# Differential attention: the two softmax maps are subtracted before they are turned and multiplied

## The chip, the cores and the metric

The kernel is one program on one core of a Trainium2 chip. TensorE (PE in the profile; its weight loads are PEld) multiplies and transposes, VectorE (DVE), ScalarE (ACT) and GpSimd (POOL) work elementwise, and SyncE (SP) issues most DMAs. Each engine runs its own queue in order and waits on semaphores for the others. The metric is the time of one execution on the device in microseconds, the median of several runs.

## The reference

The model is a first block of two layers and a second block of two layers, on 256 tokens of width 1024, all in float32. The change touches the second block alone. Each of its layers has three attentions: a latent one (MLA, 8 heads), a differential one (4 heads with two softmax maps each) and a windowed one (8 heads). The differential one is

```
s = einsum('bqmhd,bkmhd->bmhqk', qb, k) * scale
s = s - slopes[None, None, :, None, None] * dist[:, None, None]
p = softmax(s, axis=-1)
a = p[:, 0] - lam * p[:, 1]
o = einsum('bhqk,bkhd->bqhd', a, v)
...
o_diff = rms_norm(o, g_diff_out) * (1 - lam_init)
```

where m is the map (0 or 1) and h the head. After the attentions come gates (`gates = sigmoid(gate_logits)`), the three branch projections, an output projection, a feed-forward network with a convolution, and an embedding gate.

## The kernel before, in words

Weights are streamed in units of 128x1024 floats, 147 for a layer of the second block, through a ring of 7 slots. ACT rounds a unit to `w_hi` (L682), and DVE (5 of 7 units) or POOL (2 of 7) computes the rest `w_lo` (L686). PE then multiplies three times (hi by hi, hi by lo, lo by hi) for each product. In the attention stage the units of the gates are spread over the work: `gl0` to `gl23` are 24 matmuls each (L720), one unit for each step i.

The attention stage is a loop over i = 0 to 26, written out on PE, DVE and ACT alike. There are 24 items: 0 to 7 are the differential maps, 8 to 15 the windowed heads, 16 to 23 the latent heads. An item is the score matrix of one map, 256x256, held as 128x512. For an item

- PE computes the scores into a PSUM bank, two items at a time up to item 15 (`scores_pair`, L1254), one at a time after that (`scores2`, L1266);
- DVE adds the distance term into the SBUF tile `z2[:, i % 4]`, which the trace calls z (L2502), and takes the row maxima (L2507, L2509), which increments `z_ready`;
- ACT takes the exponential in place with the row sums (L1797), which increments `p_ready`;
- two steps after the item's own, PE turns the tile with four transposes into a bank (`turn2`, L1275), and ACT (even) or DVE (odd) copies it to `p_t` (`read_p2`, L575 and L573);
- three steps after its own, PE multiplies it by the values with eight matmuls (`weigh2`, L1294).

Items 0 to 3 are the first maps of the four heads and sum into the banks `od0` (0 and 1); items 4 to 7 are the second maps and sum into `od1` (2 and 3). At i = 9 and 11 DVE scales both by the reciprocal row sums, the second also by minus lambda (the name `lam[:, 2:3]` holds it with its sign), and at i = 13 it adds them, squares the sum and reduces it for the norm; at i = 17 it applies the norm (L2554 to L2576).

Beside that runs a chain for the latent heads' queries and keys (`qk`). ACT computes the inverse roots at i = 3 and 4 (L1811, `mla_rstd`), behind the exponential of the step. POOL scales each of the two token tiles twice over 1536 columns (L2794, L2798, `mla_scaled`), with its share of `w_lo` in between. DVE applies the rotary embedding in six small operations, `rope(0)` at i = 7 and `rope(1)` at i = 8 (L2523 to L2528, `mla_roped`). At i = 9 PE turns the first heads (`mla_turn`, L1307) and waits for `mla_roped` there.

PSUM has four working banks (4 to 7), handed out in turn by the table `banks2`, in the order in which PE fills them: scores, turned tiles, `gl` and the rest. A use of a bank waits until the use before it was read. What reads `gl{i}` is ACT, at the end of its step i (L1430).

## Time and profile before

| | us |
|---|---|
| median of 3 runs | 1728.37 (1727.63 to 1729.87) |
| the profiled execution | 1727.11 |
| its span, first to last instruction | 1725.3 |
| PE busy | 1653.6 (96%) |
| DVE busy | 1170.4 (68%) |
| ACT busy | 921.4 (53%) |
| POOL busy | 441.4 (26%) |
| mean granted TensorE clock | 0.986 of full speed |

The attention stage of the second block runs from about 821 to 947 us in its first layer (called layer 0 below) and from about 1306 to 1435 us in its second (layer 1). The times below are us from the start of the span. A timeline row gives start and length, and in brackets the engine's idle time before it and who ended it. Consecutive operations on DVE overlap a little: the next one starts some 0.1 us before the recorded end of the one before. The clock is granted to TensorE in two levels, 2.4 GHz (1.00 in the views) and 1.2 GHz; values in between are means over a stretch.

### The profile page before, as it was taken

The page shows a single profiled execution, that of the slowest core. Times are in us where ns is not written, and L with a number is a line of the kernel's source. Part 1 is how long each engine was busy: PE and PEld are TensorE (multiplying, and loading weights), DVE is VectorE, ACT ScalarE, POOL GpSimd, SP SyncE. Part 2 cuts the span into 40 slices and gives each one's busy share as a digit, 9 for nine tenths or more (in the row PEclk, how much of TensorE's full clock was granted, in tenths as well). Part 3 has the DMA queues.
Part 4 walks back from the last instruction along what each step waited for, and adds up shares of the span by engine and source line. Part 5 has one row for each costly group of instructions (what it writes and reads, how often), then busy time and mean ns, then how long its engine had stood idle before and what let it go on. Part 6 is the DMA issues. An engine that isn't in the chain of part 4 may idle for free.

```text
span 1725.3 us, 30143 instructions
## 1 busy us (share of the span) xinstructions
PE 1653.6 (96%) x11354; PEld 1504.2 (87%) x11354; DVE 1170.4 (68%) x1601; ACT 921.4 (53%) x1576; POOL 441.4 (26%) x184
## 2 busy tenths in 40 slices
PE   8989999999988999999999999999999999999997
PEld 6878799989887899978899989999788999899996
DVE  5687754467786545476884877666767856777677
ACT  5664554446645544465655564545755555554445
POOL 2212122212121322224511132222235211222222
PEclk9999999999999999999999999999999999999999
DMA  9432455646523665546333455655554333466653
GB/s 332 157 119 96 161 199 185 201 147 210 162 78 122 220 193 188 191 153 213 113 110 100 140 199 184 215 185 182 180 194 146 110 100 116 161 218 199 207 183 127
DMA packets 82563, 288.74 MB, mean 167 GB/s; under 512 B 9051, under 2 KB 11908, under 8 KB 81924
## 3 DMA queue, kind: packets, MB, share of 16 engines
q1 hardware_dynamic: 77352, 272.58, 48.1%
q10 hardware_dynamic: 5084, 14.37, 2.5%
q8 instruction: 91, 1.49, 0.4%
q14 instruction: 36, 0.29, 0.1%
HBM read 284.81 MB, written 2.11 MB: 166 GB/s over the span
## 4 chain that ended last, share of the span: by engine, by line
PE 62%; DVE 7%; ACT 3%; issue 2%; DVEq 0%; ACTq 0%
PE bank L720 30%; PE bank L737 25%; PE bank L1294 2%; DVE w_lo L686 2%; PE bank L1275 1%; PE bank L1266 1%; ACT w_hi L682 1%; PE bank L765 1%; PE bank L1254 1%; PE bank L1307 0%; DVE qk L2528 0%; PE bank L1186 0%; PE bank L774 0%; PE bank L910 0%; DVE z L2502 0%
## 5 line engine op out<-in xcount | busy, mean ns | idle before, releaser
L686 POOL TENSOR_TENSOR w_lo<-raw,w_hi 128x1024 fp32r<-128x1024 f32 x146 | 375.3, 2570 | 1175.7 <-ACT w_hi L682 1175.7
L686 DVE TENSOR_TENSOR w_lo<-raw,w_hi 128x1024 fp32r<-128x1024 f32 x364 | 558.2, 1558 | 153.9 <-ACT w_hi L682 151.5
L682 ACT ACTIVATE w_hi<-raw 128x1024 fp32r<-128x1024 f32 x510 | 520.0, 1052 | 101.6 <-PE bank L737 46.3
L720 PE MATMUL bank<-x_t_hi,w_hi 128*128 128x256 f32 x1984 | 321.4, 284 | 5.3 <-ACT gl L1430 2.9
L720 PE MATMUL bank<-x_t_hi,w_lo 128*128 128x256 f32 x1984 | 313.9, 280 | 0.0
L720 PE MATMUL bank<-x_t_lo,w_hi 128*128 128x256 f32 x1984 | 313.5, 280 | 0.0
L720 PEld LDWEIGHTS bank<-x_t_hi,w_hi 128*128 128x128 f32 x1984 | 273.9, 190 | 16.8 <-issue 5.1
L720 PEld LDWEIGHTS bank<-x_t_hi,w_lo 128*128 128x128 f32 x1984 | 268.7, 189 | 0.0
L720 PEld LDWEIGHTS bank<-x_t_lo,w_hi 128*128 128x128 f32 x1984 | 268.2, 189 | 0.0
L737 PE MATMUL bank<-w_hi,x_t_hi 128*128 128x512 f32 (+3 forms) x448 | 136.1, 387 | 9.4 <-issue 5.8
L737 PE MATMUL bank<-w_hi,x_t_lo 128*128 128x512 f32 (+3 forms) x448 | 133.5, 381 | 1.5 <-DVE x_t_lo L1962 1.5
L737 PE MATMUL bank<-w_lo,x_t_hi 128*128 128x512 f32 (+3 forms) x448 | 133.2, 380 | 0.0
L737 PE MATMUL bank<-w_hi,hs_hi 128*128 128x512 f32 x352 | 109.4, 392 | 4.0 <-ACT hs_hi L1875 4.0
L737 PE MATMUL bank<-w_lo,hs_hi 128*128 128x512 f32 x352 | 108.9, 390 | 0.0
L737 PE MATMUL bank<-w_hi,hs_lo 128*128 128x512 f32 x352 | 108.7, 390 | 0.0
L737 PEld LDWEIGHTS bank<-w_hi,x_t_hi 128*128 128x128 f32 x448 | 81.2, 191 | 31.0 <-issue 14.0
L737 PEld LDWEIGHTS bank<-w_hi,x_t_lo 128*128 128x128 f32 x448 | 82.4, 190 | 19.3 <-DVE x_t_lo L1962 3.4
L737 PEld LDWEIGHTS bank<-w_lo,x_t_hi 128*128 128x128 f32 x448 | 83.1, 191 | 16.3
L1871 ACT ACTIVATE gs<-cv 128x256 f32<-128x256 f32 x44 | 18.4, 419 | 145.9 <-DVE cv L2676 145.9
L737 PEld LDWEIGHTS bank<-w_lo,hs_hi 128*128 128x128 f32 x352 | 66.1, 188 | 14.6
L737 PEld LDWEIGHTS bank<-w_hi,hs_lo 128*128 128x128 f32 x352 | 66.1, 188 | 14.3
L2363 DVE TENSOR_TENSOR hs_lo<-hs,hs_hi 128x256 fp32r<-128x256 f32 x36 | 15.3, 425 | 86.6 <-ACT hs_hi L1654 86.6
(390 smaller groups left out, 2128.0 us busy)
## 6 DMA issues: line engine op xcount, KB each, us to landing
raw<-stream SPq DMA_DIRECT2D x511, 512.0 KB, 4.3
rows<-rows ACTq DMA_DIRECT2D x4, 1024.0 KB, 4.6
gain<-rows ACTq DMA_DIRECT2D x8, 512.0 KB, 4.6
hv_p<-hv_dram ACTq DMA_DIRECT2D x14, 256.0 KB
x<-x_in SPq DMA_DIRECT2D x2, 512.0 KB, 5.0
bias_r<-rev_dram SPq DMA_DIRECT2D x1, 1024.0 KB, 7.3
hv_dram<-hv ACTq DMA_DIRECT2D x2, 512.0 KB, 7.4
y_out<-x SPq DMA_DIRECT2D x2, 512.0 KB, 2.7
```

The source lines that it names most:

```text
L682: self.eng.activation(w_hi[:, i, :], raw[:, i, :], ACT.Copy).then_inc(hi_done.sem, 1)
L686: self.eng.tensor_tensor(w_lo[:, i, :], raw[:, i, :], w_hi[:, i, :].bitcast(F32), ALU.subtract).then_inc((lo_pool if self.part == "pool" e ...
L720: mm = pe.matmul(target, a[:, i, w0 + kt * P:w0 + (kt + 1) * P], b[:, k0 + kt, :], start=kt + k == 0, stop=k == 2 and kt == kts - 1)
L737: mm = pe.matmul(target, a[:, kt0 + j, t * P:(t + 1) * P], b[:, i, j * width + c0:j * width + c0 + cn], start=first and j + k == 0, stop=l ...
L765: mm = pe.transpose(b[:, k * P:(k + 1) * P], source[:, t, (4 * h + k) * P:(4 * h + k + 1) * P], ident)
L1254: mm = pe.matmul(bank[banks.bank(at, f"s{i + half}")][:, t * S:(t + 1) * S], q[:, t * P:(t + 1) * P], k, start=True, stop=True)
L1266: mm = pe.matmul(b[:, t * S:(t + 1) * S], mq_t[:, h, t * P:(t + 1) * P], mk_t[:, h, :], start=True, stop=True)
L1275: mm = pe.transpose(b[:, m * P:(m + 1) * P], z2[:, i % 4, m * P:(m + 1) * P], ident)
L1294: mm = pe.matmul(bank[b0 + t][:, o], p_t2[:, i % 2, m * P:(m + 1) * P], v, start=kk == 0, stop=kk == 1)
L1871: act.activation(gs2[:, i % 2, :], cv[:, i % 2, :], ACT.Gelu_apprx_tanh).then_inc(c["gate_silu"].sem, 1)
L2363: dve.tensor_tensor(hs_lo[:, i % TAIL, :], hs[:, i % 2, :], hs_hi[:, i % TAIL, :].bitcast(F32), ALU.subtract).then_inc(c["h_lo"].sem, 1)
```

## The change

The items 0 to 7 are reordered, so that a group of four holds both maps of two heads: items 0 and 1 are the first maps of heads 0 and 1, items 2 and 3 their second maps, items 4 to 7 the same of heads 2 and 3. After a group has its exponentials, DVE runs `mix`: reciprocals of the eight row sums, the factor lambda on four of them, four multiplications of the first maps in place and four multiply-adds that leave the difference in the slot of the second map. Only the four differences are turned and weighed; turned tiles are now counted by u = 0 to 19. The differences u = 0, 1 are turned at i = 5 and u = 2, 3 at i = 9, and weighed at i = 6, 7, 10 and 11. All four heads sum into one pair of banks `od`. The squares for its norm move from DVE to ACT at i = 12 (two activations of 128x512), and the norm is applied on the way out of the banks at i = 17. The pieces of DVE at i = 9, 11 and 13 that scaled, added and squared are gone.

```
+DIFF_TILE = [0, 2, 1, 3]
+WEIGHED = 20
+TURN_AT = {5: (0, 1), 9: (2, 3), **{u + 6: (u,) for u in range(4, WEIGHED)}}
+WEIGH_AT = {6: (0,), 7: (1,), 10: (2,), 11: (3, 4), **{u + 7: (u,) for u in range(5, WEIGHED)}}
...
-        if i >= 2:
-            work(f"p{i - 2}")
+        work(*[f"p{u}" for u in TURN_AT.get(i, ())])
...
-    out.extend([("od0", 0), ("od1", 2), ("owin", 0), ("omla", 2)])
+    out.extend([("od", 0), ("owin", 2), ("omla", 0)])
...
-                def turn2(i):
-                    pe.wait_ge(*c["p_ready"](at, i + 1))
-                    pe.wait_ge(*banks.free(at, f"p{i}"))
+                def turn2(u):
+                    if u < 4:
+                        slot = 2 + u % 2
+                        pe.wait_ge(*c["mixed"](at, u + 1))
+                    else:
+                        slot = u % 4
+                        pe.wait_ge(*c["p_ready"](at, u + 5))
+                    pe.wait_ge(*banks.free(at, f"p{u}"))
...
+                    if i == 12:
+                        act.wait_ge(*banks.full(at, "od"))
+                        for t in range(T):
+                            ins = act.activation(sq2[:, t, :], bank[t][:], ACT.Square)
+                        ins.then_inc(c["od_squares"].sem, 1)
...
-                    if i >= 4:
-                        dve.wait_ge(*banks.full(at, f"p{i - 4}"))
+                    if i in (4, 5, 8, 9):
+                        dve.wait_ge(*c["mixed"](at, i // 4 * 2))
+                    elif i >= 4:
+                        dve.wait_ge(*banks.full(at, f"p{i - 8 if i >= 12 else (i - 6) // 4 * 2 + i % 2}"))
...
+                def mix(g):
+                    r = sums2[:, 8 * g:8 * g + 8]
+                    dve.wait_ge(*c["p_ready"](at, 4 * g + 4))
+                    step(dve.reciprocal(r, r))
+                    step(dve.tensor_scalar(r[:, 4:8], r[:, 4:8], lam[:, 2:3], None, ALU.mult))
+                    for h in range(2):
+                        for t in range(T):
+                            v = z2[:, h, t * S:(t + 1) * S]
+                            ins = dve.tensor_scalar(v, v, r[:, 2 * h + t:2 * h + t + 1], None, ALU.mult)
+                    step(ins)
+                    for h in range(2):
+                        for t in range(T):
+                            v, w = (z2[:, n, t * S:(t + 1) * S] for n in (2 + h, h))
+                            ins = dve.scalar_tensor_tensor(v, v, r[:, 4 + 2 * h + t:5 + 2 * h + t], w, ALU.mult, ALU.add)
+                        ins.then_inc(c["mixed"].sem, 1)
...
+                    if i in (4, 8):
+                        mix(i // 4 - 1)
                     if i < MLA and i % 2 == 0:
                         item(i)
                         item(i + 1)
...
-                    if i == 9:
...
-                    if i == 11:
...
                     if i == 13:
-                        dve.wait_ge(*banks.read(at, "od1"))
-                        od = o3[:, :, 512:1024]
-                        step(dve.tensor_tensor(od, od, sq2[:], ALU.add))
-                        step(dve.tensor_tensor(sq2[:], od, od, ALU.mult))
+                        dve.wait_ge(*c["od_squares"](at, 1))
...
```

Three places of the order of instructions follow, each before and after, with what each instruction waits for. On PE at i = 5, before: the turn of item 3 (L1275), the weighing of item 2 (L1294), the turn of `skn` (L1186) and the start of `gl5` (L720).

```order
L1275 MATMUL bank<-consts,z_119 128x128 [waits bank_free6,p_ready]
L1275 MATMUL bank<-consts,z_119 128x128 x3
L1294 MATMUL bank<-dv,p_t_121 128x128 [waits bank_free4]
L1294 MATMUL bank<-dv,p_t_121 128x128 x3
L1186 MATMUL bank<-consts,skn 128x128 [waits head_ready,bank_free7]
L1186 MATMUL bank<-consts,skn 128x128
L720 MATMUL bank<-x_t_hi,w_hi 128x256 [waits lo_dve,bank_free4]
```

Changed, the same step: two turns that wait for `mixed`, the turn of `skn` and the start of `gl5` (now L725).

```order
L1286 MATMUL bank<-consts,z_119 128x128 [waits bank_free7,mixed]
L1286 MATMUL bank<-consts,z_119 128x128 x3
L1286 MATMUL bank<-consts,z_119 128x128 [waits bank_free4,mixed]
L1286 MATMUL bank<-consts,z_119 128x128 x3
L1191 MATMUL bank<-consts,skn 128x128 [waits head_ready,bank_free5]
L1191 MATMUL bank<-consts,skn 128x128
L725 MATMUL bank<-x_t_hi,w_hi 128x256 [waits lo_dve,bank_free6]
L725 MATMUL bank<-x_t_hi,w_hi 128x256 x3
```

Both turned differences now stand in front of `gl5`, the weighing is gone from the step, and the banks have moved on: the second turn waits for bank 4, which item 4's scores hold, `skn` for bank 5 of item 5's scores, and `gl5` for bank 6, in which `gl4` lies.

On DVE from i = 3 to 4, before: the copy of a turned tile, the read of `sqn`, one unit's `w_lo`, and items 4 and 5.

```order
L573 COPY p_t_121<-bank 128x512 [waits bank_full6]
L2422 TENSOR_SCALAR sq_t<-bank,param_66 128x512 [waits bank_full4]
L686 TENSOR_TENSOR w_lo<-raw,w_hi 128x1024 [waits hi_done]
L2502 SCALAR_TENSOR_TENSOR z_119<-dist,bank 128x512 [waits bank_full4,bank_full6]
L2507 TENSOR_REDUCE small_126<-z_119 128x2 [waits bank_free6]
L2502 SCALAR_TENSOR_TENSOR z_119<-dist,bank 128x512 [waits bank_full6,bank_full7]
L2507 TENSOR_REDUCE small_126<-z_119 128x2 [waits bank_free7]
L686 TENSOR_TENSOR w_lo<-raw,w_hi 128x1024 [waits hi_done]
```

Changed: the copy is gone, and `mix` (L2554 to L2564) stands between the `w_lo` and items 4 and 5 (L2522 and L2527).

```order
L2439 TENSOR_SCALAR sq_t<-bank,param_66 128x512 [waits bank_full6]
L691 TENSOR_TENSOR w_lo<-raw,w_hi 128x1024 [waits hi_done]
L2554 RECIPROCAL small_126<-small_126 128x8 [waits p_ready]
L2555 TENSOR_SCALAR small_126<-small_126 128x4 [waits dve_step]
L2559 TENSOR_SCALAR z_119<-z_119,small_126 128x256 [waits dve_step]
L2559 TENSOR_SCALAR z_119<-z_119,small_126 128x256 x3
L2564 SCALAR_TENSOR_TENSOR z_119<-z_119,small_126 128x256 [waits dve_step]
L2564 SCALAR_TENSOR_TENSOR z_119<-z_119,small_126 128x256 x3
L2522 SCALAR_TENSOR_TENSOR z_119<-dist,bank 128x512 [waits mixed,bank_full4]
L2527 TENSOR_REDUCE small_126<-z_119 128x2 [waits bank_free4]
L2522 SCALAR_TENSOR_TENSOR z_119<-dist,bank 128x512 [waits mixed,bank_full5]
L2527 TENSOR_REDUCE small_126<-z_119 128x2 [waits bank_free5]
```

The additions of items 4 and 5 now stand behind ten more instructions.

On DVE from the end of i = 7 to 8, before: `w_lo`, items 8 and 9, then the first of `rope(1)`'s six operations (L2523).

```order
L686 TENSOR_TENSOR w_lo<-raw,w_hi 128x1024 [waits hi_done,dve_step]
L2502 SCALAR_TENSOR_TENSOR z_119<-dist_w,bank 128x512 [waits bank_full7]
L2509 TENSOR_REDUCE small_126<-z_119 128x2 [waits bank_free7]
L2510 TENSOR_SCALAR small_126<-small_126,param_66 128x2 [waits dve_step]
L2502 SCALAR_TENSOR_TENSOR z_119<-dist_w,bank 128x512 [waits bank_full5,bank_full4]
L2509 TENSOR_REDUCE small_126<-z_119 128x2 [waits bank_free4]
L2510 TENSOR_SCALAR small_126<-small_126,param_66 128x2 [waits dve_step]
L2523 TENSOR_TENSOR rot<-qk,rope_cs 128x256 [waits mla_scaled]
```

Changed, from the same `w_lo` on: the second `mix`, then items 8 and 9 (up to their fifth row), behind which `rope(1)` follows as before.

```order
L691 TENSOR_TENSOR w_lo<-raw,w_hi 128x1024 [waits hi_done,dve_step]
L2554 RECIPROCAL small_126<-small_126 128x8 [waits p_ready]
L2555 TENSOR_SCALAR small_126<-small_126 128x4 [waits dve_step]
L2559 TENSOR_SCALAR z_119<-z_119,small_126 128x256 [waits dve_step]
L2559 TENSOR_SCALAR z_119<-z_119,small_126 128x256 x3
L2564 SCALAR_TENSOR_TENSOR z_119<-z_119,small_126 128x256 [waits dve_step]
L2564 SCALAR_TENSOR_TENSOR z_119<-z_119,small_126 128x256 x3
L2522 SCALAR_TENSOR_TENSOR z_119<-dist_w,bank 128x512 [waits mixed,bank_full7]
L2529 TENSOR_REDUCE small_126<-z_119 128x2 [waits bank_free7]
L2530 TENSOR_SCALAR small_126<-small_126,param_66 128x2 [waits dve_step]
L2522 SCALAR_TENSOR_TENSOR z_119<-dist_w,bank 128x512 [waits mixed,bank_full4]
L2529 TENSOR_REDUCE small_126<-z_119 128x2 [waits bank_free4]
```

The second `mix` has come in ahead of items 8 and 9, and so ahead of `rope(1)`.

## Rows read from the trace of the kernel before

**Rows 1.** The page, part 4: share of the chain that ended last, by engine.

```profile
PE 62%; DVE 7%; ACT 3%; issue 2%; DVEq 0%; ACTq 0%
```

**Rows 2.** Windows: engines' busy time, granted clock (PEclk), DMA share, GB/s.

```profile
903.00:947.00 44.00, 44.00 (x357) 42.67 (x356) 18.88 (x32) 22.76 (x55) 4.71 (x2) 1.00 0.32 108
...
1314.00:1318.40 4.40, 1.78 (x12) 1.18 (x12) 4.33 (x6) 4.40 (x13) 2.36 (x1) 0.82 0.33 133
1318.40:1324.00 5.60, 5.55 (x27) 5.55 (x28) 2.69 (x3) 2.50 (x7) 0.00 (x0) 0.53 0.32 94
```

**Rows 3.** Chain of waits, layers 0 and 1: start, length, engine, line, count.

```profile
833.38 3.08 PE bank L720 x24
...
841.47 1.06 PE bank L1254 x8
...
843.12 0.89 PE bank L1294 x8
844.01 2.81 PE bank L720 x24
846.82 0.44 PE bank L1275 x4
...
868.88 1.08 PE bank L1307 x8
...
1318.45 5.42 PE bank L720 x24
```

**Rows 4.** Timeline of PE: start, length, line, tiles, count, idle before.

```profile
831.28 0.63 PE L1275 MATMUL bank<-consts,z 128*128 128x128 f32 x4 [0.61 <-ACT gl L1430]
```

**Rows 5.** Timeline of POOL, layer 0.

```profile
838.38 2.76 POOL L2794 TENSOR_TENSOR qk<-qk,small 128x1536 f32<-128x1536 f32 x1 [5.08 <-ACT small L1811]
841.22 4.34 POOL L2798 TENSOR_TENSOR qk<-qk,param 128x1536 f32<-128x1536 f32 x1
...
849.40 3.74 POOL L2794 TENSOR_TENSOR qk<-qk,small 128x1536 f32<-128x1536 f32 x1
853.22 3.51 POOL L2798 TENSOR_TENSOR qk<-qk,param 128x1536 f32<-128x1536 f32 x1
859.24 2.63 POOL L686 TENSOR_TENSOR w_lo<-raw,w_hi 128x1024 fp32r<-128x1024 f32 x1 [2.51 <-ACT w_hi L682]
```

**Rows 6.** Timeline of DVE, layer 0.

```profile
834.31 1.74 DVE L2544 TENSOR_REDUCE small<-mla_sq 128x16 f32<-128x1536 f32 x1
...
839.37 2.85 DVE L686 TENSOR_TENSOR w_lo<-raw,w_hi 128x1024 fp32r<-128x1024 f32 x1
...
843.28 0.69 DVE L2507 TENSOR_REDUCE small<-z 128x2 f32<-128x512 f32 x1
...
859.57 2.59 DVE L2528 TENSOR_TENSOR qk<-qk,rot 128x256 f32<-128x256 f32 x1
...
863.34 0.68 DVE L2502 SCALAR_TENSOR_TENSOR z<-dist_w,bank 128x512 f32<-128x512 f32 x1
...
866.49 0.42 DVE L2523 TENSOR_TENSOR rot<-qk,rope_cs 128x256 f32<-128x256 f32 x1
```

**Rows 7.** Timeline of ACT, layer 0.

```profile
834.22 0.58 ACT L575 ACTIVATE p_t<-bank 128x512 f32<-128x512 f32 x1
...
836.50 0.38 ACT L1430 ACTIVATE gl<-bank 128x256 f32<-128x256 f32 x1 [0.75 <-PE bank L720]
...
838.09 0.22 ACT L1811 ACTIVATE small<-small 128x16 f32<-128x16 f32 x1
```

**Rows 8.** Lines L2173, L2199: min/median/max ns, first and last start.

```profile
L2173 DVE TENSOR_SCALAR t<-t,lbc x8: 405/407/416, 91.9 to 455.7; 128x256 f32<-128x256 f32 x8
...
L2199 DVE SCALAR_TENSOR_TENSOR log_f<-log_f,lbc,t x8: 476/482/2632, 102.8 to 466.8; 128x256 f32<-128x256 f32 x8
```

**Rows 9.** Timelines of DVE and POOL in the first block.

```profile
57.27 1.67 DVE L2154 TENSOR_SCALAR gates<-gates 128x48 f32<-128x48 f32 x1
...
56.50 2.40 POOL L686 TENSOR_TENSOR w_lo<-raw,w_hi 128x1024 fp32r<-128x1024 f32 x1 [15.41 <-ACT w_hi L682]
```

More of the change, by code:

```diff
@@ L283 @@
     qk_act=(0, 1), qk_dve=(0, 1), mla_squared=(0, 2), mla_ms=(0, 2), mla_rstd=(0, 2), mla_scaled=(0, 2),
-    mla_roped=(0, 1), od_squared=(0, 1), od_rstd=(0, 1), sink_in=(0, 1), sink_exp=(0, 1), o3_ready=(0, 1),
+    mla_roped=(0, 1), od_squares=(0, 1), od_squared=(0, 1), mixed=(0, 4), od_rstd=(0, 1), sink_in=(0, 1), sink_exp=(0, 1), o3_ready=(0, 1),
     gate_sig=(0, 8), merge_ready=(0, 8), merge_hi=(0, 8), merge_lo=(0, 8), conv_ready=(0, 22),
@@ L1268, in scores2, with weigh2 @@
                     mm.then_inc(*banks.fills(at, f"s{i}"))
-                def turn2(i):
-                    pe.wait_ge(*c["p_ready"](at, i + 1))
-                    pe.wait_ge(*banks.free(at, f"p{i}"))
-                    b = bank[banks.bank(at, f"p{i}")]
-                    for m in range(4):
-                        mm = pe.transpose(b[:, m * P:(m + 1) * P], z2[:, i % 4, m * P:(m + 1) * P], ident)
-                    mm.then_inc(*banks.fills(at, f"p{i}"))
-                def weigh2(i):
-                    h = PAIRED[i % 8] if WIN <= i < MLA else i % 8
-                    name = [n for e, n in PV_ENDS.items() if i <= e][0]
+                def turn2(u):
[6 more added lines that the diff above has]
+                    pe.wait_ge(*banks.free(at, f"p{u}"))
+                    b = bank[banks.bank(at, f"p{u}")]
+                    for m in range(4):
+                        mm = pe.transpose(b[:, m * P:(m + 1) * P], z2[:, slot, m * P:(m + 1) * P], ident)
+                    mm.then_inc(*banks.fills(at, f"p{u}"))
+                def weigh2(u):
+                    h = u if u < 4 else PAIRED[u - 4] if u < 12 else u - 12
+                    name = [n for e, n in PV_ENDS.items() if u <= e][0]
                     b0 = banks.bank(at, name)
-                    if i in (0, 4, 8, 16):
+                    if u in (0, 4, 12):
                         pe.wait_ge(*banks.free(at, name))
-                    pe.wait_ge(*banks.read(at, f"p{i}"))
+                    pe.wait_ge(*banks.read(at, f"p{u}"))
                     for t in range(T):
                         for kk in range(T):
-                            if i < WIN:
-                                v, o = dv[:, kk, (i % 4) * P:(i % 4 + 1) * P], slice((i % 4) * P, (i % 4 + 1) * P)
-                            elif i < MLA:
+                            if u < 4:
+                                v, o = dv[:, kk, h * P:(h + 1) * P], slice(h * P, (h + 1) * P)
+                            elif u < 12:
                                 v, o = sv[:, kk, 64 * (h // 4):64 * (h // 4) + 64], slice(64 * h, 64 * h + 64)
@@ L1293, in weigh2 @@
                             m = t * 2 + kk
-                            mm = pe.matmul(bank[b0 + t][:, o], p_t2[:, i % 2, m * P:(m + 1) * P], v,
+                            mm = pe.matmul(bank[b0 + t][:, o], p_t2[:, u % 2, m * P:(m + 1) * P], v,
                                            start=kk == 0, stop=kk == 1)
-                    if i in PV_ENDS:
+                    if u in PV_ENDS:
                         mm.then_inc(*banks.fills(at, name))
@@ L1316, in second_block @@
                         scores2(i)
-                    if 2 <= i < ITEMS + 2:
-                        turn2(i - 2)
-                    if i >= 3:
-                        weigh2(i - 3)
+                    for u in TURN_AT.get(i, ()):
+                        turn2(u)
+                    for u in WEIGH_AT.get(i, ()):
+                        weigh2(u)
                     if i in MLA_TURNS:
@@ L1803, in second_block @@
                             act.nop().then_inc(*banks.frees(at, f"s{i}"))
-                    if i >= 2 and i % 2 == 0:
-                        read_p2(act, at, i - 2)
+                    for u in TURN_AT.get(i, ()):
+                        if u % 2 == 0:
+                            read_p2(act, at, u)
+                    if i == 12:
[3 more added lines that the diff above has]
+                        ins.then_inc(c["od_squares"].sem, 1)
                     if i == 3 or i == 4:
@@ L2536, in second_block @@
                         item(i)
-                    if i >= 3 and i % 2 == 1:
-                        read_p2(dve, at, i - 2)
+                    for u in TURN_AT.get(i, ()):
+                        if u % 2 == 1:
+                            read_p2(dve, at, u)
                     if i == 3:
```

29 lines of the change are left out of this document (9 added, 20 removed).

## The prediction

> **What bounds the kernel now.** I read the page's chain first, then the chain in order of time, then the timelines of the attention stage engine by engine. PE carries 62% of the chain, DVE 7% [rows 1]. The second half of the attention stage is pure PE: from 903 to 947 us it is busy 44.00 of 44.00 us, with DVE at 18.88 and POOL at 4.71 [rows 2]. The first half (i = 2 to 9) is not. A step there is a chain of PE pieces, 1.06 us scores, 0.44 turn, 0.89 weigh, 2.81 gate unit [rows 3], but it ends at PE's first turn of the latent heads at 868.88 [rows 3], which had to wait for `rope(1)` on DVE (from 866.49 [rows 6]). PE stood still 1.06 us there, so before the change the two sides arrive nearly together. That is what matters: whatever PE saves before i = 9 is worth nothing unless the chain to `mla_roped` also gets shorter.
>
> **PE's part.** Per layer four turns of 0.44 and four weighings of 0.89 go [rows 3], 1.8 + 3.6 = 5.3 us, 10.6 us in two layers. Up to i = 9 five weighings are gone, one of which comes back at i = 11 (two in one step), behind the wait for `mla_roped`. So if that wait decides, PE's saving is zero and the one moved back costs +0.9 per layer. One more gain: `gl2` now takes the bank for which the first turn waited, so it can start at 831.28 [rows 4] and not at 833.38 [rows 3].
>
> **The chain to `mla_roped`, first half.** Take layer 0 and start at 831.28. PE: `gl2` 3.08 to 834.4, two turns of `sqn` 0.9 (as two of 0.44), `gl3` 2.81, scores 1.06, `gl4` 2.81 [rows 3]: at 841.9 PE is at i = 5 and wants the first difference. DVE: the reduction ends at 836.05 [rows 6], the read of `sqn` takes some 0.7, so `w_lo` runs from 836.7 to about 837.9. ACT no longer copies a turned tile (0.58) nor waits 0.75 for `gl2`, so the inverse root that ends at 838.31 is there at 837.0 [rows 7], and POOL's L2794, which starts at 838.38 [rows 5], asks for its data at 837.05, in the middle of that `w_lo`.
>
> Now the shared data path. In the trace DVE operations that read SBUF twice stand still for as long as a POOL operation runs: `w_lo` at 839.37 ends at 842.22, 1.1 us behind POOL's end at 841.14, and L2528, 256 columns, starts at 859.57 and ends at 862.16, 0.3 us behind POOL's end at 861.87 [rows 5, 6]. The other way round, L2798 takes 3.51 alone and 4.34 when a `w_lo` got in first, L2794 2.76 alone and 3.74 [rows 5]. An operation with one SBUF source and a scalar does it too: L2154, 48 columns, takes 1.67 us and ends at 58.94, POOL's at 58.90 [rows 9]. And a POOL operation that asks while DVE works gets in between two DVE operations: the `w_lo` at 859.24 came between L2527 and L2528. `mix` consists of just such operations: four of the kind of L2173 (407 ns with two scalars, some 0.3 us from start to start) and four of the kind of L2199 (482 ns, some 0.4) [rows 8], with 0.45 for the two small ones: 3.2 us undisturbed. Old items 4 and 5, which read z's summand from PSUM, were never held.
>
> So: POOL's L2794 ends at 837.05 + 3.74 = 840.8; `mix`, ready at 838.4, gets one multiplication in; L2798, which has asked by then, takes 3.5 to 844.6; the other three and the four multiply-adds follow, to 847.2. The first difference is there at 846.4, 4.5 us after PE wanted it.
>
> The Trainium skill, "SBUF — State Buffer", section "SBUF: two separate sides", says the same as a rule: VectorE in a two-port mode or with two SBUF inputs and GpSimd hold a shared port pair exclusively, and whoever starts first keeps it for the whole instruction. By this rule all eight big operations of `mix` can be held, as I assume; if it did not hold for the multiplications, the second rival below would be the sum.
>
> **Second half.** Item 4's maxima come 1.4 us behind `mix`, at 848.6, against 843.97 before [rows 6]: +4.6. Behind them in ACT's queue stand the exponential, then the second inverse root (without the 0.58 copy), so POOL's second pair is late by 4.05, and L2798, which ended at 856.73 [rows 5], ends at 860.8. `gl4`'s bank is read by ACT only behind that exponential, the inverse root and a `w_hi`, some 3 us after the maxima, so PE's `gl5` starts near 851.5: PE stands idle some 8 of the 9.6 us from 841.9. It keeps clear of the chain behind that: scores 6 and 7 are there before 858. DVE then: `rope(0)` 2.3 from 860.8 (as `rope(1)`, 866.49 to PE's 868.88), POOL's next `w_lo` falls into it as before (+2.4), `w_lo` 1.2, the second `mix` 3.2, items 8 and 9 3.15 (863.34 to 866.49), `rope(1)` 2.35 [rows 5, 6]: 875.3. That is +6.4 against 868.88.
>
> **Later and elsewhere.** DVE loses four pieces of 1.2 to 1.7 us at i = 9 to 13 and ACT gains 1.2 at i = 12; both lie beside a PE that is busy throughout [rows 2], worth nothing. If ACT's cover were thin there, it would cost at most those 1.2 us. `od` is freed at i = 17, near seven us before the latent sums need its bank: nothing.
>
> The clock. In layer 1 PE was busy 1.78 of 4.40 us from 1314, and the granted clock then was 0.53 from 1318.4 to 1324 [rows 2]: `gl2` took 5.42 instead of 3.08 [rows 3], 2.34 lost, in a stretch that ran on PE. With `gl2` two us earlier, and with the DVE chain as the bound, this loss is no longer there: -2.34 once. But eight us of idle PE at i = 5 and again at i = 9 (PE arrives near 868, `mla_roped` at 875) will bring the lower level too. Behind i = 5 it is covered by the wait at i = 9; behind i = 9 nothing covers it: 0 to 2.34 a layer, I take 2.0, near the one row there is.
>
> **Sum.** Layer 0: 6.4 + 0.9 + 2.0 = +9.3. Layer 1: the same less 2.34 = +7.0. Together +16.3 on the profiled execution's 1727.11 (span 1725.3, 1.8 around it): 1743.4. That execution lies 1.3 below the median of 1728.37 and within its three runs' spread; I say 1743.
>
> **The rivals.**
> - The lock does not hold `mix` up. Then `mix` ends at 841.1, item 4's maxima at 842.5, 1.5 earlier than before, POOL's second pair ends near 854.7. But `rope(0)`, held till then and by the next `w_lo`, ends near 859.5, and `w_lo`, `mix` (3.2), items 8 and 9 and `rope(1)` end at 869.4: the same as before within half a us. +0.9 a layer, clock +4.0 - 2.34: +3.5, 1730.6. For it: no row has a 256-column multiplication under a POOL operation. Against it: L2154.
> - PE stays the bound, and its removed work simply comes off: -10.6, and -2.34 for the clock, 1714. It needs `mla_roped` before about 863, which asks for a POOL pair five us earlier or no second `mix` ahead of `rope(1)`. Against it: DVE's queue.
> - The second `mix` is held too. POOL's `w_lo`, 2.4 us, falls behind `rope(0)`, or PE's idle at i = 5 costs more than the slack of 2 us behind it: +2.5 to 3 a layer, 1749.
> - The change gives nothing at all since the savings on both sides cancel, as if both chains met in the middle: between the last two signs, 1727.
>
> **How the numbers follow.** What can be told from no change in this kernel is about 0.2%, 3.5 us, so the same is 1725 to 1732. My forecast 0.52; the lock not holding 0.17, of which half lies beyond 1732; PE's saving 0.11; the second held 0.13; cancelling 0.07. Faster 0.12, same 0.15, slower 0.73. Range: from 1727, where the cancelling case lies, to 1752, the held case and its clock; the likeliest case alone has 1736 to 1749, since its clock term may be 0 and the tie at 840.8 may go to DVE (-3.5 a layer, in part hidden).
>
> **What would show it.** Right: one of L2559 or L2564 near 3.5 us long in each layer while L2798 runs; PE's longest idle times in the stage at the turn of the first difference, `gl5` waiting for ACT's `gl`, and the first turn of `qk` (near 875 and 1360), each of several us; PE's granted clock below 1.00 behind them; from i = 10 on steps as before. Step by step wrong: `mix` 3.2 us long in both layers (no lock); PE reaching the turn of `qk` without a wait (PE bound). The forecast as a whole falls if `mla_roped` comes before 869 in layer 0.

## The result, and the profile after

The changed kernel takes 1744.14 us (median of 5 runs, 1742.95 to 1746.0), the kernel before 1728.37 (1725.13 to 1729.87) beside it: a ratio of 1.0094, 95% interval 1.0082 to 1.0107. The forecast was 1743. The profiled execution is 1744.56, its span 1742.8.

The page, part 4 (shares of the chain that ended last), which answers to [rows 1]:

```profile
PE 60%; DVE 10%; ACT 2%; issue 2%; DVEq 0%; ACTq 0%
```

DVE has gone from 7% to 10% of the chain. PE is busy 1654.8 us as before (1653.6), although 10.6 us of its work are gone: part of the rest ran at half clock (mean granted clock 0.978, before 0.986). Windows of the changed kernel: all engines in the steady stretch that answers to [rows 2]; then PE alone (busy time, clock, DMA share, GB/s) where [rows 2] had 0.53, and behind the two long waits:

```profile
913.00:957.00 44.00, 44.00 (x357) 42.67 (x355) 18.85 (x33) 22.74 (x55) 4.71 (x2) 1.00 0.33 108
```

```profile
1329.00:1335.00 6.00, 6.00 (x52) 1.00 0.29 91
851.90:857.20 5.30, 5.29 (x26) 0.54 0.46 133
875.50:882.00 6.50, 6.42 (x34) 0.60 0.47 163
```

Behind the weighing moved to i = 11 nothing has changed: from the scores of i = 12 to those of i = 14 both kernels take 10.31 us. Layer 1's drop at `gl2` is gone, and two others have come in each layer. PE of the changed kernel, layer 0 (start, length, line, count, idle time before; L1286 turns a map, L1318 `qk`, L725 is a gate unit):

```profile
846.81 1.11 PE L1286 MATMUL bank<-consts,z 128*128 128x128 f32 x4 [3.89 <-DVE z L2564]
848.49 1.09 PE L1286 MATMUL bank<-consts,z 128*128 128x128 f32 x4 [0.57 <-DVE z L2522]
851.91 1.22 PE L725 MATMUL bank<-x_t_hi,w_hi 128*128 128x256 f32 x4 [1.50 <-ACT gl L1441]
...
875.58 1.94 PE L1318 MATMUL bank<-consts,qk 128*96 128x128 f32 x8 [4.09 <-DVE qk L2548]
```

The same four waits stand in layer 1. VectorE beside it, then POOL, layer 0; they answer to [rows 6] and [rows 5]:

```profile
838.68 0.19 DVE L2554 RECIPROCAL small<-small 128x8 f32<-128x8 f32 x1
838.91 2.49 DVE L2555 TENSOR_SCALAR small<-small 128x4 f32<-128x4 f32 x1
841.44 4.40 DVE L2559 TENSOR_SCALAR z<-z,small 128x256 f32<-128x256 f32 x4
845.87 1.67 DVE L2564 SCALAR_TENSOR_TENSOR z<-z,small 128x256 f32<-128x256 f32 x4
...
864.93 2.10 DVE L2555 TENSOR_SCALAR small<-small 128x4 f32<-128x4 f32 x1
```

```profile
837.95 3.42 POOL L2815 TENSOR_TENSOR qk<-qk,small 128x1536 f32<-128x1536 f32 x1 [3.69 <-ACT small L1828]
841.45 3.45 POOL L2819 TENSOR_TENSOR qk<-qk,param 128x1536 f32<-128x1536 f32 x1
...
853.99 3.75 POOL L2815 TENSOR_TENSOR qk<-qk,small 128x1536 f32<-128x1536 f32 x1
857.82 3.49 POOL L2819 TENSOR_TENSOR qk<-qk,param 128x1536 f32<-128x1536 f32 x1
864.56 2.44 POOL L691 TENSOR_TENSOR w_lo<-raw,w_hi 128x1024 fp32r<-128x1024 f32 x1 [3.24 <-ACT w_hi L687]
```

The four-column L2555 ends at 841.40, right behind POOL's L2815 (841.37); it gets in between POOL's two operations. The first of the four L2559 lasts 3.61 us, till 0.15 us behind L2819's end at 844.90 (the shortest takes 0.34). The second mix's L2555 ends at 867.03, behind POOL's `w_lo` (867.00).

Where the 17.5 us between the two spans lie: 0.9 ahead of the stage; 5.8 in layer 0 from the scores of items 2 and 3 to the turn of `qk` (829.53 to 868.88 before, 830.45 to 875.58 now); 3.2 in layer 0 behind that turn (`qk` at 1.94 instead of 1.08 and the gate unit behind it at 4.28 instead of 2.83, 2.3 together, and the weighing moved to i = 11, 0.9); 1.0 between the layers, which I did not trace; 3.5 in layer 1's same stretch (1314.60 to 1356.27 before, 1325.51 to 1370.66 now), which held the old drop of 2.3; 3.1 behind it. The 0.9 and the 1.0 lie outside the changed stage, so they are not shown to come from the change.

### The profile page after: what moved, and what is told of

Same layout as the page of the kernel before. It is cut to its first block, busy times and chain, and to the rows that moved or that the text cites. A ratio compares the mean times of both kernels' runs of the same rounds, so it can differ in the third digit from the quotient of the medians.

```text
span 1742.8 us, 29953 instructions
## 1 busy us (share of the span) xinstructions
PE 1654.8 (95%) x11258; PEld 1503.4 (86%) x11258; DVE 1177.0 (68%) x1621; ACT 919.3 (53%) x1576; POOL 438.7 (25%) x184
## 4 chain that ended last, share of the span: by engine, by line
PE 60%; DVE 10%; ACT 2%; issue 2%; DVEq 0%; ACTq 0%
PE bank L725 29%; PE bank L742 25%; DVE w_lo L691 2%; PE bank L1305 2%; PE bank L1286 1%; PE bank L1271 1%; ACT w_hi L687 1%; DVE z L2522 1%; PE bank L770 1%; DVE z L2559 1%; DVE small L2555 1%; PE bank L1318 1%; PE bank L779 1%; PE bank L1259 0%; DVE small L2527 0%
## 5 line engine op out<-in xcount | busy, mean ns | idle before, releaser
L725 PE MATMUL bank<-x_t_hi,w_hi 128*128 128x256 f32 x1984 | 324.3, 286 | 5.7 <-ACT gl L1441 4.0
L725 PE MATMUL bank<-x_t_hi,w_lo 128*128 128x256 f32 x1984 | 315.4, 281 | 0.0
L725 PE MATMUL bank<-x_t_lo,w_hi 128*128 128x256 f32 x1984 | 314.3, 281 | 0.0
L725 PEld LDWEIGHTS bank<-x_t_hi,w_hi 128*128 128x128 f32 x1984 | 276.6, 191 | 20.2 <-issue 6.6
L725 PEld LDWEIGHTS bank<-x_t_hi,w_lo 128*128 128x128 f32 x1984 | 270.4, 191 | 0.0
L725 PEld LDWEIGHTS bank<-x_t_lo,w_hi 128*128 128x128 f32 x1984 | 269.2, 190 | 0.0
L742 PEld LDWEIGHTS bank<-w_lo,x_t_hi 128*128 128x128 f32 x448 | 83.2, 191 | 16.3
```

What stands on the lines that cost most here:

```text
L725: mm = pe.matmul(target, a[:, i, w0 + kt * P:w0 + (kt + 1) * P], b[:, k0 + kt, :], start=kt + k == 0, stop=k == 2 and kt == kts - 1)
L742: mm = pe.matmul(target, a[:, kt0 + j, t * P:(t + 1) * P], b[:, i, j * width + c0:j * width + c0 + cn], start=first and j + k == 0, stop=l ...
```

## The experiments

Twelve kernels, each beside runs of the kernel before on the same chip. They were run on three chips: the kernel before took 1727.63 us beside the first four rows below the changed kernel's, 1726.54 beside the next four and 1727.51 beside the last four. Kernels of different groups are best compared by their ratios. The stretch is the one above, from the scores of items 2 and 3 to the turn of `qk` in layer 0, in each kernel's own profile; it is one execution and not the median.

| kernel | median us | ratio to before (95%) | stretch us |
|---|---|---|---|
| before | | | 39.35 |
| changed | 1744.14 | 1.0094 (1.0082 to 1.0107) | 45.13 |
| POOL's first pair left out | 1735.71 | 1.0053 (1.0035 to 1.0071) | 40.56 |
| mix left out | 1723.56 | 0.9979 (0.9970 to 0.9989) | 35.91 |
| folded mix | 1737.82 | 1.0069 (1.0050 to 1.0088) | 43.25 |
| second rotation first | 1745.61 | 1.0118 (1.0096 to 1.0140) | 44.54 |
| POOL waits | 1736.44 | 1.0056 (1.0040 to 1.0073) | 42.66 |
| PE kept busy, two places | 1742.83 | 1.0091 (1.0074 to 1.0108) | 47.52 |
| folded, POOL waits | 1735.29 | 1.0051 (1.0034 to 1.0067) | 40.36 |
| folded, earlier roots | 1729.45 | 1.0017 (1.0007 to 1.0026) | 38.41 |
| PE kept busy, six places | 1739.26 | 1.0071 (1.0054 to 1.0087) | 45.18 |
| folded, earlier roots, lighter POOL | 1723.45 | 0.9975 (0.9965 to 0.9985) | 34.55 |
| before, earlier roots, lighter POOL | 1727.37 | 1.0003 (0.9994 to 1.0013) | 39.32 |
| changed, earlier roots, lighter POOL | 1743.42 | 1.0100 (1.0083 to 1.0117) | 44.52 |

**POOL's first pair left out.**

```diff
+                    if t == 0:
+                        split.ahead(uid["gl3"])
+                        pool.nop().then_inc(c["mla_scaled"].sem, 1)
+                        continue
```

> POOL's two operations that scale the first token tile of qk (L2815 and L2819 with t = 0) are left out, so that half of the MLA queries and keys stays unscaled; all else is the changed kernel. Theory of the held path (VectorE's operations on SBUF wait for the POOL operation that runs): with no POOL operation between 838 and 845 in layer 0, L2555 falls from 2.49 to about 0.23 us and the four L2559 from 4.40 to about 1.14; the first difference is ready near 841.5, before PE asks for it at 842.9, so the 3.9 us of PE's wait there and the 1.5 us behind it go in both layers; the items behind are earlier by 4.4 us, POOL's second pair with them, and mla_roped comes near 871 in place of 875.5: about 4.4 us a layer, 1735. Rival, the length of VectorE's queue alone: the durations of L2555 and L2559 stay as they are and so does the time, 1743 to 1745. Rival, the granted clock: it stays as it was behind the turn of qk, where a wait of 4 us remains, so no more than 1 us of the gain comes from it.

1735.71. The timeline of VectorE in this kernel:

```profile
839.26 0.23 DVE L2555 TENSOR_SCALAR small<-small 128x4 f32<-128x4 f32 x1
839.53 1.14 DVE L2559 TENSOR_SCALAR z<-z,small 128x256 f32<-128x256 f32 x4
840.71 1.67 DVE L2564 SCALAR_TENSOR_TENSOR z<-z,small 128x256 f32<-128x256 f32 x4
```

The same instructions in the same order take 3.0 us instead of 8.6 when POOL is quiet, and PE's wait for the first difference is gone. The theory of the held path gave both the durations and the time; queue length alone is out. One part of the expectation failed: the wait of 1.5 us behind that first wait, for ACT's `gl`, is still there (1.58).

**Mix left out.**

```diff
-                    r = sums2[:, 8 * g:8 * g + 8]
                     dve.wait_ge(*c["p_ready"](at, 4 * g + 4))
...
+                    dve.nop().then_inc(c["mixed"].sem, 2)
```

> The differences are not formed: VectorE's eighteen-odd operations of mix are left out, and the second maps of each head are turned in their place, unnormalised. PE, POOL, ACT and the order of all else are the changed kernel's. This prices mix as a whole, with what it holds up. Theory that mix (its own length and the hold) is all that costs: mla_roped comes near 866, about when PE asks for the turn of qk, and nearly the whole of PE's saving of 5.3 us a layer shows, 1714 to 1720. Rival, POOL's scaling of the second tile bounds mla_roped in any case (its pair ends no earlier than 857, and the first rotation, items 8 and 9 and the second rotation come behind it): 1720 to 1728. Rival, something else in the change costs the time (the weighing moved to i = 11, the earlier gl2, the squares on ACT): it stays above 1735.

1723.56, in the first rival's range: PE still waits at the turn of `qk`. Mix as a whole, with what it holds up, costs some 20 us of the changed kernel; the hold on the first mix is 7 to 8 of them by the run before this one. Its waits in this kernel, layer 0 (for what, us in total, times, longest):

```profile
PE bank L1318 <- DVE qk L2548: 4.1, 1, 4.1
PE bank L1259 <- DVE z L2522: 1.3, 1, 1.3
PE bank L1286 <- DVE z L2522: 1.2, 1, 1.2
```

The first rotation is held by POOL's second pair till 857.7, as that rival has it, and by POOL's next `w_lo` till 860.2, but that is not the whole of it. From `w_lo` on, VectorE needs 1.2 + 3.15 + 2.35 us for items 8 and 9 and the second rotation. Before, PE had two turns and two weighings beside that (2.7 us); the change took the two weighings (1.8 us), and the time became a wait. Even a mix that cost nothing is worth 3.4 us of PE's 5.3 in this stretch, less 2.0 for the clock behind the wait (5.85 us from the turn of `qk` to the scores of i = 10, 3.85 before). So this order did not reach the 1714 of a PE-bound kernel even without mix.

**Folded mix.** The ratio is formed instead of two inverses; 1 / sum_a is put back at i = 13 and 17.

```diff
-                    step(dve.reciprocal(r, r))
-                    step(dve.tensor_scalar(r[:, 4:8], r[:, 4:8], lam[:, 2:3], None, ALU.mult))
-                    (the four tensor_scalar over z2)
+                    step(dve.reciprocal(r[:, 4:8], r[:, 4:8]))
+                    step(dve.scalar_tensor_tensor(r[:, 4:8], r[:, 4:8], lam[:, 2:3], r[:, 0:4], ALU.mult, ALU.mult))
...
+                        for n in range(2):
+                            step(dve.tensor_tensor(od_v, od_v, sa_v, ALU.mult))
```

> The first map's normalisation is taken out of mix: z_b * (-lambda * sum_a / sum_b) + z_a is formed, the four TENSOR_SCALARs over 256 columns go, the ratio is one SCALAR_TENSOR_TENSOR of 4 columns, and 1 / sum_a is put back on the 8 columns of mean squares and of their roots (four small operations a layer at i = 13 and 17). The whole computation is done. Theory of the held path: the small operation and the four L2564 are 1.9 us; at worst one of them waits for POOL's L2815 to end at 841.4, so the first difference stands at 842 to 843.2, where PE asks at 842.9; the second mix is shorter by 1.1 to 3 us; mla_roped near 868 to 869: 7 us a layer less than the changed kernel, 1730 (1726 to 1734). Rival, SCALAR_TENSOR_TENSORs wait for each POOL operation too: one is held by L2819 till 844.9 and the gain is 3 us a layer, 1737. Rival, queue length alone: only the 1.14 us and so of the multiplications go, 1740 to 1742.

1737.82: the first rival. VectorE, layer 0:

```profile
838.35 2.51 DVE L2558 SCALAR_TENSOR_TENSOR small<-small 128x4 f32<-128x4 f32 x1
840.90 4.94 DVE L2562 SCALAR_TENSOR_TENSOR z<-z,small 128x256 f32<-128x256 f32 x4
```

Held just as the TENSOR_SCALARs were: four columns for 2.3 us, and the four big ones for 3.3 us more. My expectation rested on only one of them being held; fewer operations do not help while POOL's pair lies in the same place.

**Second rotation first.**

```diff
+                    if i == 8:
+                        rope(1).then_inc(c["mla_roped"].sem, 1)
                     if i in (4, 8):
                         mix(i // 4 - 1)
```

> In the changed kernel VectorE's second rotation (i = 8) is put ahead of the second mix and of items 8 and 9; nothing is added or left out. Theory that mla_roped sets the end of the stage: it now comes near 869.3 (the rotation itself is held by POOL's w_lo till 867.0), PE's wait of 4.1 us at the turn of qk goes, and one of 2.8 us comes in its place at the turn of the third difference, which is ready near 872.5; with 0 to 1.5 us of clock 1.3 to 3 us a layer are gained, 1738 to 1741.5. Rival, that the order does not matter since both waits sum to the same queue: 1744. Rival, that items 8 and 9 now come too late for PE and ACT: 1746 to 1748.

1745.61, a miss. PE in this kernel, layer 0:

```profile
870.39 0.66 PE L1286 MATMUL bank<-consts,z 128*128 128x128 f32 x4 [1.83 <-DVE z L2564]
872.07 0.74 PE L1286 MATMUL bank<-consts,z 128*128 128x128 f32 x4 [1.02 <-DVE z L2522]
873.65 1.06 PE L1318 MATMUL bank<-consts,qk 128*96 128x128 f32 x4 [0.84 <-DVE z L2522]
875.31 1.09 PE L1318 MATMUL bank<-consts,qk 128*96 128x128 f32 x4 [0.60 <-ACT gl L1441]
```

The one wait of 4.1 us came apart into four of 4.3 together, and the clock was no better: the gate unit behind them again begins with 1.22 us for four matmuls. Its 44.54 us in the table end at the first half of the turn of `qk`; the second half starts 1.66 us later. The rival that the order does not matter had 1744, and the interval of the ratio overlaps that of the changed kernel. Both orders are the same VectorE work between the same points, with one hold by POOL's `w_lo`; it fell on the rotation here, and the mix's four-column L2555 took 0.23:

```profile
863.34 2.60 DVE L2543 TENSOR_TENSOR rot<-qk,rope_cs 128x256 f32<-128x256 f32 x1
```

**POOL waits.** Nothing removed: POOL scales the first tile behind the mix.

```diff
+                    if t == 0:
+                        pool.wait_ge(*c["mixed"](at, 2))
                     step(pool.tensor_tensor(qk[:, t], qk[:, t], mla_ms[...
```

> The changed kernel, with one wait more: POOL waits for the first mix to end before it scales the first token tile of qk (L2815, t = 0). Nothing is left out. Theory of the held path: L2555 0.23 and the four L2559 1.14 as in the run without that pair, the first difference near 841.5, POOL's first pair 841.6 to 848.6, its second near 851 to 858.3; VectorE's first rotation ends where POOL's second pair lets it, near 860.5, and mla_roped near 871: 1735.7, the same as with the pair left out. Rival, it was the work of the pair and not its place that cost: 1742 to 1745.

1736.44. VectorE and POOL:

```profile
837.64 0.23 DVE L2555 TENSOR_SCALAR small<-small 128x4 f32<-128x4 f32 x1
837.90 1.14 DVE L2559 TENSOR_SCALAR z<-z,small 128x256 f32<-128x256 f32 x4
839.08 1.67 DVE L2564 SCALAR_TENSOR_TENSOR z<-z,small 128x256 f32<-128x256 f32 x4
840.87 0.69 DVE L2522 SCALAR_TENSOR_TENSOR z<-dist,bank 128x512 f32<-128x512 f32 x1
```

```profile
840.90 2.76 POOL L2817 TENSOR_TENSOR qk<-qk,small 128x1536 f32<-128x1536 f32 x1 [7.90 <-DVE z L2564]
843.73 4.33 POOL L2821 TENSOR_TENSOR qk<-qk,param 128x1536 f32<-128x1536 f32 x1
```

One added wait makes the changed kernel some 7 us faster (7.7 by the medians, 6.6 by the ratios), and the medians do not tell it from the kernel with the pair left out: it was mainly where the pair stood that cost. The work of the pair shows in the stretch, which is 2.1 us longer here than without it; `mla_roped` came at 871.8, the rotation being held by POOL's displaced second pair. And a form that is not held is seen here: L2522, whose second source is a PSUM bank, takes 0.69 us with POOL at work.

**Folded, POOL waits.** The two edits together.

> The folded mix (ratio, four SCALAR_TENSOR_TENSORs, 1 / sum_a put back later) together with POOL's wait for the first mix. The whole computation is done. Held path theory: the first mix is 2.1 us, the first difference at 840.5; the first rotation is bound by POOL's second pair as in the run with POOL's wait alone (near 860.5), and the second mix is shorter by 1.1 us: about 1 us a layer less than that run, 1733 to 1734; the wait of PE at the turn of qk still 3 us. Rival, the two gains add in full (3.1 + 4.3 us a layer): 1729.

1735.29, above the 1733 to 1734 expected and far from the rival's 1729. The stretch is 2.3 us shorter than with the wait alone, the time only 1.2 us, within the two intervals. The gains do not add in full; how much they add stays open.

**PE kept busy, two places.**

```diff
+                    if u == 0:
+                        pe.wait_ge(*banks.free(at, "p0"))
+                        for n in range(32):
+                            pe.transpose(bank[banks.bank(at, "p0")][:, 0:P], ident, ident)
```

> The changed kernel, with PE kept at work in its two longest idle times: 32 extra turns of the identity into the bank of the first difference before it waits for it (3.5 us for an idle time of 3.9), and 36 into the bank of the first qk turn (for 4.1); they are overwritten. Theory that the granted clock drops behind these idle times: the eight L1318 fall from 1.94 to 1.08 and the gl matmuls behind them from 4.28 to 2.81, the first gl behind the difference from about 5.3 to nearer 2.9, so items 6 and 7 no longer wait 3.1 us; since POOL's second pair ends at 861.3 all the same, the first rotation gains 0.5 us or less, and the whole gain is 2.3 to 3 us a layer: 1738 to 1739.5. If the drop between i = 5 and 7 fed into mla_roped after all: 6 us a layer, 1732. Rival, the drop does not hang on the idle time: 1744 or, with the filling running late, up to 1746.

1742.83, a miss by my own sizing: the ratio of 1.0091 is the changed kernel's (1.0094) within its interval. The 36 extra turns at i = 9 ran in part at half clock (0.70 on average), behind waits of 1.0 and 0.9 us, and lasted 5.73 us, over the wait they were to fill. `gl5` still began at half clock (0.50), behind waits of 0.38, 1.03, 0.60 and 1.75 us with short pieces of work between them, and with 3.65 us of extra turns at full clock ahead of the first.

**PE kept busy, six places.** The same helper ahead of each turn, `gl5` and the turn of `qk`.

```diff
+                    fill(f"p{u}", {0: 32, 1: 4, 2: 3, 3: 5}.get(u, 0))
...
+                            fill("mt0", 28)
                             pe.wait_ge(*c["mla_roped"](at, 1))
```

> The changed kernel, with PE kept at work in every idle time from the first difference to the turn of qk: extra turns of the identity into the bank that PE fills next, 32, 4, 3 and 5 of them ahead of the four turns of differences, 14 ahead of gl5 and 28 ahead of the turn of qk; they are overwritten. The first filling left short idle times of 1.0, 0.6 and 1.8 us, gl5 stayed at half clock (1.23 us for four matmuls) and the 36 turns at i = 9 themselves ran at 0.16 us each and ended late. Theory that the short idle times in a row are enough for the drop: gl5's first four matmuls fall from 1.22 to 0.74, items 6 and 7 wait 1 us or less, the turn of qk runs at 1.1 us for eight and the gl behind it at 2.8: 2.3 to 2.8 us a layer, 1738.5 to 1740. Rival, the clock is lost ahead of the idle times and filling does not bring it back: 1742 to 1745.

1739.26. The chain of waits' gate units at i = 5 and 9, then the turn of `qk`:

```profile
855.24 2.81 PE bank L725 x24
878.26 2.81 PE bank L725 x24
```

```profile
877.18 1.08 PE L1325 MATMUL bank<-consts,qk 128*96 128x128 f32 x8
```

Full clock throughout (granted clock 1.00 from 848 to 881), and 4.9 us less than the changed kernel in two layers, 4.0 by the ratios. The profiled execution is the longest of its four (1743.8). The stretch to the turn of `qk` is unchanged (45.18 against 45.13), although items 6 and 7 came 0.7 us earlier: the first rotation was held by POOL's second pair till the same point. So `gl5`'s slow start (5.26 us instead of 2.81) costs nothing in the end. From the turn of `qk` to the scores of i = 10 it is 3.82 us instead of 6.15, so the drop at i = 9 costs 2.3 us a layer in the trace and 2.0 to 2.4 by the times.

**Folded, earlier roots.** The folded mix and POOL's wait for the first mix stay. ACT forms the two roots one item earlier, POOL does one operation ahead of mix and three in a row behind it, before its `w_lo`.

```diff
-                    if i == 3 or i == 4:
-                        t = i - 3
+                    if i == 2 or i == 3:
+                        t = i - 2
```

> The folded mix; ACT computes the roots for MLA's two token tiles one item earlier each (behind the maps 2 and 3); POOL does its first scaling operation before mix, waits for mix, then does the other three in a row, ahead of its w_lo for gl4's units. The whole computation is done. Theory that POOL's second pair behind the first rotation bounds mla_roped in the run without mix (1723.6): the pair ends near 853 in place of 861, the first rotation runs unheld at 853 to 856, the second mix, items 8 and 9 and the second rotation end near 865, when PE asks for it at 866; PE bounds the stage, its idle times of over 1 us go and with them the half clock: 1715 to 1722. Rival, PE's i = 7 to 9 hold items 8 and 9 and so the second rotation to 867 or later in any case: 1722 to 1727. Rival, POOL's w_lo comes too late for PE: 1730.

1729.45, against an expectation of 1715 to 1722. The rival of 1730 is met in number only: it had PE waiting for POOL's `w_lo`, and PE's waits here are for z, `gl` and `qk` (4.09 us at the turn). The rotation is still held, VectorE of this kernel:

```profile
851.71 2.61 DVE L2544 TENSOR_TENSOR rot<-qk,rope_cs 128x256 f32<-128x256 f32 x1
854.36 2.48 DVE L2545 TENSOR_TENSOR qk<-qk,rope_cs 128x256 f32<-128x256 f32 x1
```

POOL's pair was done, at 851.5, but its two `w_lo` that had stood back for the pair followed (851.47 to 856.55). VectorE never idles from 834 to 868.

**Folded, earlier roots, lighter POOL**, and the same two edits on the kernel before and on the changed kernel as it is.

```diff
-                    step(pool.tensor_tensor(qk[:, t], qk[:, t], mla_ms[:, 16 * t:16 * t + 16].unsqueeze(2)
-                                            .broadcast_to([P, 16, 96]), ALU.mult))
+                    step(pool.tensor_tensor(qk[:, t, 8:16], qk[:, t, 8:16], mla_ms[:, 16 * t + 8:16 * t + 16].unsqueeze(2)
+                                            .broadcast_to([P, 8, 96]), ALU.mult))
...
+                    q, k = qk[:, t, 0:8, 64:96], qk[:, t, 8:16]
```

> The folded mix, POOL's wait and ACT's earlier roots as in the run before, and less work for POOL: the queries' roots go into the scale of ACT's exponentials (and into the negated maxima on VectorE) and are no more multiplied on POOL, and the queries' gain on the 64 unrotated dimensions goes into the keys' gain; POOL then multiplies 768, 256 and 768 columns a tile in place of 1536 and 1536. The whole computation is done. Theory that VectorE's operations with two SBUF sources and POOL's together fill the stretch from 834 to 867 (in the run with the earlier roots VectorE was never idle there and 8 us of it were waits for POOL): about 5.5 us of POOL's go, VectorE ends the second rotation 4 us earlier, near 862.5, where PE asks for it: 1719 to 1723. Rival, PE's scores of items 8 and 9 come first now: no more than 2 us a layer, 1725 to 1727.

> The kernel before, with ACT's earlier roots and POOL's lighter scaling (as in the run with the folded mix), and nothing of the change. PE waits only 1.06 us for the rotation there, so that is nearly all there is to gain, with the half clock of layer 1 (2.3 us in all) if its waits go as well: 1722 to 1725. Rival, the lighter scaling helps as much as in the changed kernel (4 us a layer): 1718.

> The changed kernel with the same two edits and its own mix, unfolded and without POOL's wait. Against the kernel before with these edits it is the change alone, once POOL holds VectorE less. Theory of the held path: L2555 and L2559 wait for operations of 0.7 to 2 us in place of 3.4, mla_roped comes near 866: 1724 to 1728, 0 to 4 us above the kernel before with these edits. Rival, queue length: 1738 or more. Rival, PE's 5.3 us a layer now show: 10 us below that kernel, 1714.

The first, 1723.45, beats both kernels: 0.25% under the one before (0.15 to 0.35%), 1.2% under the changed one. It is 0.5 us above the 1719 to 1723 expected, no difference that could be told; PE still waits 3.5 us at the turn of `qk`, and the second mix still meets POOL's `w_lo` in layer 0 (a four-column operation of 2.25 us). The second, 1727.37, is a miss, against 1722 to 1725 and a rival of 1718: no measurable difference. POOL's scaling is done at 844.3 there and not at 856.7, but PE still waits 1.06 us at the turn of `qk`. The first rotation stands behind the copy of a turned tile as before, and its last operation is held by the same `w_lo` of POOL:

```profile
859.52 2.59 DVE L2533 TENSOR_TENSOR qk<-qk,rot 128x256 f32<-128x256 f32 x1
```

The third was a plain miss: 1743.42. The number lies in the range of the rival of queue length (1738 or more), but the rows show holds and not a longer queue. Its VectorE and POOL, layer 0:

```profile
838.37 1.56 DVE L2560 TENSOR_SCALAR small<-small 128x4 f32<-128x4 f32 x1
839.97 4.40 DVE L2564 TENSOR_SCALAR z<-z,small 128x256 f32<-128x256 f32 x4
...
863.21 2.30 DVE L2560 TENSOR_SCALAR small<-small 128x4 f32<-128x4 f32 x1
```

```profile
839.87 1.47 POOL L2821 TENSOR_TENSOR qk<-qk,small 128x768 f32<-128x768 f32 x1
841.42 0.73 POOL L2826 TENSOR_TENSOR qk<-qk,param 128x256 f32<-128x256 f32 x1
842.11 1.85 POOL L2827 TENSOR_TENSOR qk<-qk,param 128x768 f32<-128x768 f32 x1
```

POOL's six short operations stand in a row now, and the four multiplications lose 3.3 us to them just as to one long one: the first three of the four L2564 take 1.52, 0.89 and 1.89, one held by each of POOL's three operations here, and the fourth 0.34. PE comes late to items 6 and 7 as before (VectorE waits 3.45 us for it), and the second mix meets POOL's `w_lo` again. Less work on POOL without moving it out of the mix's way is worth nothing; with the wait and the fold it is worth 6 us (7 by the ratios) against the same kernel with POOL's full scaling.

## Why the prediction was right

The forecast of 1743 held, and so did its main cause, by its own steps; the times of the changed kernel are given here less the 0.92 us by which its stage starts later.

- **PE's saving is worth nothing before i = 9**: right. PE arrives early and waits 4.09 us at the turn of `qk`. Of the time from the end of `gl4` to `gl5` it was idle 6.1 of 9.0 us, not 8 of 9.6: the turns between ran at half clock. The run without mix adds what I had not seen: PE's removed work was itself the cover of items 8 and 9 and of the second rotation.
- **`gl2` two us earlier, no drop in layer 1**: right, the clock is 1.00 there, and layer 1's stretch grew 2.3 us less than layer 0's (3.5 against 5.8).
- **POOL holds the first mix by one L2798 of 3.5 us**: right in kind and sum, wrong in one detail. One L2559 stood for 3.3 us while L2819 ran. But what got in between POOL's two operations was the four-column L2555, which itself had waited 2.3 us for L2815, not one of the multiplications. First difference 845.8 against 846.4 predicted, item 4's maxima 848.2 against 848.6.
- **POOL's second pair to 860.8**: 860.4. **`gl5` near 851.5**: 851.0, behind ACT.
- **`mla_roped` at 875.3**: 874.6, but two of its terms changed places. I let the first rotation be held by POOL's `w_lo`; it was the second mix's L2555 instead, for the same 2 us. So my third rival's mechanism, the second mix held too, did happen, in the place of a hold and not on top of one. And VectorE waited 3.1 us for the scores of items 6 and 7, which PE brought at half clock. They were there at 857.3, before 858 as said, but the slack was not the 2 us that my third rival had: VectorE was through with them only 0.3 us before POOL's pair ended. So the late scores cost nothing, but only just.
- **Clock 2.0 a layer at i = 9**: 2.3 in the trace, 2.0 to 2.4 by the run with PE kept busy in six places. **The weighing moved**: 0.9, as said.
- **Sum**: +16.3 predicted on the profiled execution, +17.5 measured. The terms that the prediction named come to 15.6 in the trace (5.8 + 3.2 and 3.5 + 3.1); the other 1.9 are the 0.9 ahead of the stage and the 1.0 between the layers. Over the kernels here, whose work ahead of the stage is the same, the start of the stage lies between 828.5 and 832.5, so such sizes are not the change's. That the median came within 1.1 us of the forecast is therefore in part luck; that it rose by some 16 us is not.

The rivals fell: that the lock doesn't hold the mix, by the run without POOL's pair and the one in which POOL waits; that PE stays bound, by its waits and by the run without mix; that both savings cancel (1727), by the time itself. Where the prediction says "the second rival below" for multiplications that are not held, the first in its list is meant.

The Trainium skill, "SBUF — State Buffer", section "SBUF: two separate sides", has the rule that VectorE in a two-port mode or with two SBUF inputs, or GpSimd, whoever starts first, keeps the shared pair for its whole instruction and the other blocks. The traces agree: 2.49 us against 0.23, and 3.61 us for the longest L2559 against 0.34 for the shortest. It says of VectorE operations with two SBUF inputs that they contend with a GpSimd operation that reads SBUF; the folded mix (2.51 and 4.94 us) agrees, and L2522, with one source in PSUM, was not held (0.69).

## What to carry to other kernels

Work moved onto VectorE costs more than its own 3.2 us, by where it lands in time: look which GpSimd operations run in that stretch, and try a wait on GpSimd before you rewrite the operations. Work removed from PE while it is about to wait anyway becomes a wait, and may cost the clock behind it. And cutting the other engine's operation into short ones does not help where they stand in a row: each holds the next of yours.

## What the runs showed of the hardware beyond that

- A VectorE operation of four columns is held too: 2.49 us where it takes 0.23 alone. The RECIPROCAL of eight columns right ahead of it, in the middle of the same POOL operation, took its 0.19.
- The wait shows as busy time of the held instruction, not as idle time: POOL's hold on the mix stands in no list of waits. It is seen by comparing the instruction with the same one elsewhere.
- When both engines have operations in line, they took turns, one for one: L2555 between L2815 and L2819 in the changed kernel, and with POOL's short operations one of VectorE's L2564 behind each, however short it was itself (0.34 us) beside POOL's (0.73 to 1.85).
- PE's half clock came behind several waits of 0.4 to 1.8 us in a row, with work between them, not only behind one long one: 1.23 us for the first four matmuls of `gl5` with 3.65 us of extra turns ahead of these waits. With four more extra turns (some 0.5 us) between them, and waits of 0.42, 0.94, 0.22 and 1.75 us left, the clock stayed at 1.00 and the four took 0.72. With POOL's first pair left out, a single wait of 1.58 us stood ahead of `gl5`, and they took 0.74.
